# Second block's stick-breaking heads: activation table asked for early, absolute value read from PSUM, logits copied by VectorE

## The reference

```
def stick_breaking_attention(q, k, v):
    """A[t,s] = beta_ts * prod_{s<j<t}(1-beta_tj), s < t."""
    ...
        z = jnp.einsum('bthd,bshd->bhts', qb, k).astype(jnp.float32) * (dh ** -0.5)
        log_beta = jax.nn.log_sigmoid(z)
        log_1m = jnp.where(strict, jax.nn.log_sigmoid(-z), 0.0)
        after = lax.cumsum(log_1m, axis=3, reverse=True) - log_1m
        a = jnp.where(strict, jnp.exp(log_beta + after), 0.0)
        return jnp.einsum('bhts,bshd->bthd', a.astype(v.dtype), v)
```

## Time and profile before

| what | value |
|---|---|
| median of 3 runs | 3764.31 us |
| the profiled execution, its own time | 3760.81 us |
| its span | 3759.0 us |
| TensorE (PE) busy | 3449.2 us, 92% |
| VectorE (DVE) busy | 1741.6 us, 46% |
| ScalarE (ACT) busy | 1082.9 us, 29% |
| mean granted TensorE clock | 0.964 of full |
| stick heads, layer 1 | about 2372 to 2603 us |
| stick heads, layer 2 | about 3094 to 3326 us |

### The profile page before, as it was taken

One profiled execution on the slowest core, in us unless ns is written; L12 is line 12 of the kernel. 1 busy time (PEld: TensorE's weight loads), 2 busy tenths in 40 slices (PEclk: granted clock), 3 DMA queues, 4 the chain that ended last, 5 costly groups with the idle time before them and its releaser, 6 DMA issues. The chain is left out here.

```text
span 3759.0 us, 44273 instructions
## 1 busy us (share of the span) xinstructions
PE 3449.2 (92%) x17084; PEld 2331.7 (62%) x17084; DVE 1741.6 (46%) x3034; ACT 1082.9 (29%) x1679; POOL 38.6 (1%) x42
## 2 busy tenths in 40 slices
PE   7999996999987999996999986999999989999998
PEld 5766683444445866684444445776766767777666
DVE  7766633212235866633212134457644344666433
ACT  4343321100123333321101023444332124433321
POOL 1000000000000100000000000000000000000000
PEclk9999997999998999998999998999999989999999
DMA  5521128999944431126999962211211231212122
GB/s 196 190 81 57 64 81 337 421 424 424 423 175 143 181 113 57 52 89 272 423 424 424 423 241 85 70 62 65 93 68 68 101 110 45 72 68 88 64 93 87
DMA packets 129207, 653.55 MB, mean 174 GB/s; under 512 B 21972, under 2 KB 32212, under 8 KB 61944
## 3 DMA queue, kind: packets, MB, share of 16 engines
q1 hardware_dynamic: 129016, 650.98, 44.7%
HBM read 632.54 MB, written 14.72 MB: 172 GB/s over the span
## 5 line engine op out<-in xcount | busy, mean ns | idle before, releaser
L1629 PE MATMUL ps<-normed_T_hi,ring_split 128*128 128x512 f32 (+1 forms) x1952 | 624.6, 401 | 18.3 <-PEq L264 13.1
L1629 PEld LDWEIGHTS ps<-normed_T_hi,ring_split 128*128 128x128 f32 (+1 forms) x1952 | 363.5, 190 | 121.1 <-issue 40.4
L1629 PE MATMUL ps<-normed_T_lo,ring_split 128*128 128x512 f32 (+1 forms) x976 | 384.4, 394 | 0.0
L2274 PE MATMUL ps<-normed_T_hi,ring_split 128*128 128x512 f32 x1024 | 337.0, 411 | 8.9 <-DVE branches L2536 7.6
L1905 DVE TENSOR_TENSOR ring_split<-weight_ring,ring_split 128x2048 fp32r<-128x2048 f32 x76 | 173.9, 2289 | 167.0 <-ACT ring_split L1789 166.7
L2274 PEld LDWEIGHTS ps<-normed_T_hi,ring_split 128*128 128x128 f32 x1024 | 193.3, 192 | 82.0 <-issue 32.5
L1629 PEld LDWEIGHTS ps<-normed_T_lo,ring_split 128*128 128x128 f32 (+1 forms) x976 | 184.7, 189 | 41.2
L2274 PE MATMUL ps<-normed_T_lo,ring_split 128*128 128x512 f32 x512 | 203.1, 397 | 0.0
L1684 PE MATMUL ps<-branches 128*128 128x512 f32 x384 | 173.0, 593 | 3.3 <-issue 3.0
L1230 PE MATMUL ps<-weight_ring,projected 128*64 128x512 f32 x768 | 167.9, 593 | 0.0
L1789 ACT ACTIVATE ring_split<-weight_ring 128x2048 fp32r<-128x2048 f32 x76 | 144.7, 1909 | 65.7 <-DMA weight_ring<-in_w_slabs 58.4
(11 more groups left out here) (422 smaller groups left out, 6251.9 us busy)
## 6 DMA issues: line engine op xcount, KB each, us to landing
weight_ring<-in_w_slabs SPq DMA_DIRECT2D x78, 1024.0 KB, 4.9
weight_ring<-in_w_exp_gate SPq DMA_DIRECT2D x48, 1024.0 KB, 17.9
weight_ring<-in_w_exp_down SPq DMA_DIRECT2D x48, 1024.0 KB, 13.8
weight_ring<-in_w_exp_up SPq DMA_DIRECT2D x48, 1024.0 KB, 22.0
weight_ring<-in_w_branch_gate SPq DMA_DIRECT2D x32, 1024.0 KB, 4.9
spare_weights<-in_w_exp_up SPq DMA_DIRECT2D x32, 1024.0 KB, 22.9
spare_weights<-in_w_exp_gate SPq DMA_DIRECT2D x32, 1024.0 KB, 22.2
spare_weights<-in_w_exp_down SPq DMA_DIRECT2D x32, 1024.0 KB, 17.4
```

Of the source, the lines that this page charges most:

```text
L1629: ins = e.matmul(dst, lhs(k, m), rhs(k, m), start=k == 0 and m == 0, stop=k == KD - 1 and m == 2)
L2274: ins = e.matmul(dst, lhs(k, m), rhs(k, m), start=k == 0 and m == 0, stop=k == KD - 1 and m == 2)
```

## The change

ScalarE's `front` asks for the table `natural_log_exp_and_others` as its first act, ahead of its waits, takes the absolute value straight from PSUM, and no longer copies z. VectorE gets a new step `copy_logits` at the place of front in the list: it takes out the last dense step, waits for ScalarE's Abs, and copies z from PSUM to `wt`. `stage_a` is a semaphore that this stage did not use before.

```diff
--- before.py
+++ after.py
@@ -1348,6 +1348,7 @@
             iw = small[:, 8:24].rearrange("p (t h) -> p t h", t=NT)
             landed = [s["slab_landed_0"], s["slab_landed_1"], s["slab_landed_2"]]
             side_landed = [s["side_landed_0"], s["side_landed_1"]]
+            stick_read = s["stage_a"]
 
             steps, ready, silus = [], {}, []
             counts = {"dense_scalar": 0, "dense_vector": 0, "rotated": 0}
@@ -1834,16 +1835,13 @@
                                 merged_to_hi(7)
 
                     def front(h):
-                        e.wait_ge(s["stick_logits"], h + 1)
+                        e.preload_act_table_set("natural_log_exp_and_others")
                         v = ln[:, h % 2, :]
                         if h >= 2:
                             e.wait_ge(s["stick_sums"], h - 1)
-                            e.wait_ge(s["stick_output"], h - 1)
-                        z = wt[:, h % 2, :]
-                        e.activation(z, z_ps, ACT.Copy).then_inc(s["stick_copied"], 1)
-                        e.wait_ge(s["stick_copied"], h + 1)
-                        e.activation(v, z, ACT.Abs).then_inc(s["scalar_step"], st_.add("scalar_step"))
-                        e.wait_ge(s[st_.name], st_.value)
+                        e.wait_ge(s["stick_logits"], h + 1)
+                        e.activation(v, z_ps, ACT.Abs).then_inc(stick_read, 1)
+                        e.wait_ge(stick_read, h + 1)
                         e.activation(v, v, ACT.Exp, scale=-1.0).then_inc(s["scalar_step"], st_.add("scalar_step"))
                         e.wait_ge(s[st_.name], st_.value)
                         e.activation(v, v, ACT.Ln, bias=1.0).then_inc(s["stick_log"], 1)
@@ -1991,8 +1989,15 @@
                             e.wait_ge(s["dense_vector"], st["taken"][1])
                             inner(e.tensor_tensor(X[:, t, c], X[:, t, c], tmp_out[:, i % 2, :], ALU.add))
 
+                    def copy_logits(h):
+                        if h >= 2:
+                            e.wait_ge(s["stick_output"], h - 1)
+                        e.wait_ge(stick_read, h + 1)
+                        e.tensor_copy(wt[:, h % 2, :], z_ps).then_inc(s["stick_copied"], 1)
+
                     def after_logs(h):
                         v = ln[:, h % 2, :]
+                        e.wait_ge(s["stick_copied"], h + 1)
                         e.wait_ge(s["stick_log"], h + 1)
                         e.scalar_tensor_tensor(v, wt[:, h % 2, :], 0.0, v, ALU.max, ALU.add).then_inc(s["stick_ln"], 1)
 
@@ -2079,6 +2084,9 @@
                         if what == "dense":
                             dense(n)
                             last = n
+                        elif what == "front":
+                            evict(last)
+                            copy_logits(n)
                         elif what == "logs":
                             if n >= 2:
                                 gate_stick(n - 2)
```

## The result

The kernel after the change takes 3735.55 us (median of 4 runs, 3731.91 to 3740.26), the kernel before on the same chip 3763.41 (4 runs, 3761.83 to 3765.1). The ratio is 0.9927, with a 95% interval of 0.9909 to 0.9944: 27.9 us faster, where 25.5 were forecast. The profiled execution took 3733.84 us with a span of 3732.1, which is 26.9 us less than before; the mean granted clock rose from 0.964 to 0.967.

The account below looks back on a forecast made before the run. TensorE, busy 92% of the span, was taken as the bound, so only its waits and slow clock could be gained. 2.64 + 3.27 + 4.04 + 2.79 = 12.74 us a layer, 25.5 in two, gave 3738.8 us; 8-in-10 range 3729 to 3752.

Parts of the forecast that it names:

- The chain of the front: ScalarE's front in head 2: Copy and table load leave, 2.56 us of 6.43, so 3.87 us is left.
- Head 0: TensorE's wait for the bank that L1944 frees goes, as the front ends 3.85 us earlier: gain 2.64 us a layer.
- Heads 2 and 3: TensorE's waits for logs (1.48, 2.25 us) go, with 1.79 us of slow clock each: gains 3.27 and 4.04 us.
- Head 7: Logits wait goes; VectorE's copy leaves a 2.3 us wait at sums, 1.79 us slow clock counted against: net 2.79 us.
- Heads 1 to 6: VectorE's new copy runs beside ScalarE's Exp and Ln and costs nothing in these heads.
- The sum: Gains of heads 0, 2, 3 and 7: 12.74 us a layer, 25.5 us in two, giving 3738.8 us.
- one set of rows stands for both: Layer 2 shows layer 1's six TensorE waits within 0.35 us, so layer 1 was worked out and doubled.
- The clock holds in head 7: Rival: head 7's 2.3 us wait brings no slow clock, 3735.2 us; with VectorE ready too, 3730.6 us; chance 0.17.
- The waits go and the slow clock doesn't: Rival: only the stick heads' waits count, 7.53 us a layer, giving 3749.2 us; chance 0.15.
- Lost again behind the heads: Rival: VectorE's new copies come late in the attention that follows; half the gain goes, 3751.5 us; chance 0.06.
- The table isn't kept: Rival: the compiler loads Exp's table again, the front stays at 6.4 us, nothing gained, 3764 us; chance 0.06.
- VectorE binds every head: Rival: the copy makes heads 1 to 7 all VectorE-bound, slower at 3788 us; chance 0.06.

Follow-up runs that it names:

- the doubled copy: Kernel after the change, with VectorE's copy of the logits made twice in every head: 3742.29 us, ratio to before 0.995.
- the same edit: Kernel after, sums added onto logits in PSUM, no copy or subtract: 3751.25 us with next head's logits earlier in the list, 3719.61 us with their place kept.
- the kernels with a half of the change: Kernel before plus only the table request: 3733.05 and 3737.91 us on two chips; kernel after without the request: 3740.83 us.
- the late request: Kernel after, with the table asked for between Abs and Exp instead of ahead of the waits: 3739.73 us, ratio to before 0.9943.

## Why the prediction held, point by point

**The chain of the front** was put at 3.87 us. In head 7 Abs starts at 2567.86 and Ln ends at 2571.71, which makes 3.85. Abs from PSUM takes 1.24 us, as Copy did. The load is one a head, hidden as described.

**Head 0.** The wait of 2.64 us is gone in both layers, as said. But its price was read from layer 1 alone, where the clock stayed at 1.00. In layer 2 of the kernel before the same wait did bring the slow clock:

```profile
3111.86 0.73 PE L1629 MATMUL ps<-normed_T_hi,ring_split 128*128 128x512 f32 x2 [2.64 <-DVE projected L1944]
...
3112.66 0.94 PE L1629 MATMUL ps<-normed_T_hi,ring_split 128*128 128x512 f32 x2
```

```profile
3111.00:3117.00 6.00, 5.13 (x16) 4.07 (x16) 5.41 (x7) 0.00 (x0) 0.00 (x0) 0.72 0.38 156
```

The granted clock is 0.72 over these 6 us. The second row shows a pair of matmuls at 0.94 us; undisturbed pairs of this kind take 0.61 or 0.62. Besides, head 0's sums start 22.8 us after its logits in layer 1 and 24.4 us in layer 2. That was another 1.6 us to be had.

**Heads 2 and 3.** Waits and slow clock went, sums at 4.60 and 4.55 us against the 4.50 I used. The 0.3 us to spare in head 3 were enough.

**Head 7.** The copy was costed at 1.48 us and takes 1.49; VectorE's run at 27.25 + 1.48 = 28.73 us and measures 28.66; TensorE's wait at 2.3 us and is 2.17; the wait at the logits is gone. The slow clock counted against it is there in layer 1 (6.28 us) and not in layer 2 (4.60).

**Heads 1 to 6.** The copy costs nothing there, as argued, but head 1's old wait of 0.75 us was followed in layer 1 of this profile by the slow clock: 1.05 us for the four small logits matmuls against 0.66 in layer 2, and a granted clock of 0.86 over 12 us:

```profile
2398.00:2410.00 12.00, 11.21 (x43) 7.97 (x40) 7.01 (x10) 9.86 (x12) 0.00 (x0) 0.86 0.01 2
```

12 x 0.14 = 1.7 us lost, where I had counted none.

**The sum.** From head 0's logits to head 7's last weigh, layer 1 is 11.6 us shorter, where 12.74 were forecast; head 1's new slow clock is the difference and a little more. Layer 2 is 16.0 us shorter. That is 12.74, plus 1.8 for head 7 without the slow clock, plus 1.6 for head 0 in layer 2, which is 0.1 too much. Between the layers 1.1 us was lost again: TensorE's wait for its own sequencer (L264) grew from 6.5 us to 7.9, and others shrank a little. 11.6 + 16.0 - 1.1 = 26.5 us, and the span shrank by 26.9; most of the rest was gained behind the heads. The step that failed is "one set of rows stands for both": it holds for the waits, to 0.35 us, and not for the clock behind them. Three clock terms of 1.6 to 1.8 us, two in favour and one against, were off by it, and they came to no more than 2 us because their signs differed. That the sum came so near is luck to that extent; the waits and the chain were right without it.

**The rivals.** "The clock holds in head 7" came true in one layer of two. "The waits go and the slow clock doesn't" fell with the sums of heads 2 and 3. "Lost again behind the heads" came true for 1.1 us. "The table isn't kept" fell with 16 loads at L1838 and none at L1845, L1847 or L1851. "VectorE binds every head" fell; it binds head 7 alone, and the doubled copy shows that even 3 us a head would add only one more head to it.

What the prediction did not see is how little of the change was needed. It added the two savings, 1.27 and 1.29 us, to one chain and compared their sum with each wait. It never asked what each would do alone, and the rows would have told most of it: head 2's wait of 1.48 us and head 7's 2.43 us come down by one load, 1.28 and 1.16 us, to 0.2 and 1.27 by the table request alone, with no copy in VectorE's run.

## What to carry to other kernels

An activation table can be asked for before the wait that its function stands behind; where ScalarE idles there, that one line takes the load off the chain, and it gave here 27.4 and 24.5 us on two chips, nearly all of what the whole change gave (27.9 and 27.4 on one chip each). Price a shorter chain wait by wait and each part of the change alone, since two savings on one chain don't add once the waits are used up, and what is moved to another engine is paid where that engine works without a gap. When a step is taken out of a list that is placed by cost, keep its place in the list, and compare the two lists before the two times: the same edit gave 3751.25 and 3719.61 us.

## What the runs showed of the hardware that I had not expected

How long TensorE waits doesn't tell whether the slow clock follows. In the kernel before a wait of 2.64 us brought it in one layer and not in the other; in the kernel after 2.17 us did so in layer 1 and not in layer 2, in three profiles of three; 1.27 us did in both layers of one profile and in neither of the next of the same kernel; even 0.75 us did in four of six places of the kernel after, in two of the eight of the kernels with a half of the change or the late request, and in neither layer of the kernel before. When it comes it costs 1.6 to 1.8 us in most places here and up to 3.4, more than some of the waits themselves, so a wait is best priced with it and without it. Two kernels that differ by a few microseconds can differ by this alone. I did not find what decides.

A table load costs its 1.28 us and a gap of 0.01 or 0.02 us, whether it stands between Exp and Ln (kernel before), between Abs and Exp (late request) or ahead of Abs (kernel after). And matmuls that add onto logits already in PSUM cost what those that start anew do, 4.60 us for the 20.
